# A three-stage attention kernel: new orders for scores, maxima, exponentials, values and the ring of three banks, own PSUM banks for the short rows, and q/k loads a head ahead of v

## What is computed

```python
s = einsum('qd,kd->qk', q, k) * 64 ** -0.5     # forgetting attention: + c[q] - c[k], causal
s = where(mask, s, -inf)                        # sparse: top-256 keys; dilated: three windows
m = max(s, -1); e = exp(s - m); den = sum(e, -1)
o = einsum('qk,kd->qd', e, v) / den
```

## Time and profile before

| what | value |
| --- | --- |
| median of 3 runs | 3623.88 us (3623.08 to 3627.99) |
| the profiled execution | 3628.1 us, its span 3626.3 us |
| mean granted TensorE clock | 0.961 of full |
| TensorE matmul busy | 3270.4 us (90%) |
| TensorE weight load busy | 2684.2 us (74%) |
| VectorE busy | 1818.7 us (50%) |
| ScalarE busy | 1278.6 us (35%) |
| GpSimd busy | 821.7 us (23%) |
| stretch of the FOX stage | about 587 to 765 us |
| stretch of the sparse stage | about 763 to 950 us |
| stretch of the dilated stage | about 2254 to 2596 us |

### The profile page before, as it was taken

The page is one execution under the profiler, slowest core; times in us unless marked ns, Lnnn a source line. Parts: engine busy times, 40 slices in busy tenths (PEclk is TensorE's granted clock), DMA queues, the critical chain, the costliest instruction groups (busy, mean ns, idle before and its releaser), DMA issues. The chain is left out here.

```text
span 3626.3 us, 45156 instructions
## 1 busy us (share of the span) xinstructions
PE 3270.4 (90%) x15622; PEld 2684.2 (74%) x15622; DVE 1818.7 (50%) x3077; ACT 1278.6 (35%) x2732; POOL 821.7 (23%) x509
## 2 busy tenths in 40 slices
PE   8778986969889999999988998799888999999988
PEld 6556875857667888888866886677677888888866
DVE  2398994748424444444442431688524444444342
ACT  3364424747423222222232211677513221222231
POOL 2332264345211000000031441666211000000030
PEclk9899998989989999999999999899998999999999
DMA  4203222212212111111021223222112111111021
GB/s 131 53 16 104 93 90 82 47 41 59 82 47 82 47 35 58 46 35 58 0 76 38 93 98 128 52 49 55 53 42 58 58 46 49 46 44 58 0 76 47
DMA packets 268629, 214.78 MB, mean 59 GB/s; under 512 B 95164, under 2 KB 220908, under 8 KB 268524
## 3 DMA queue, kind: packets, MB, share of 16 engines
q1 hardware_dynamic: 268524, 213.43, 19.9%
HBM read 170.93 MB, written 41.94 MB: 59 GB/s over the span
## 5 line engine op out<-in xcount | busy, mean ns | idle before, releaser
L67 PE MATMUL l0in_acc<-l0in_w_lo,l0h_hi 128*128 128x512 f32 x384 | 151.9, 395 | 25.0 <-POOL l0in_w_lo L1581 25.0
L1655 DVE TENSOR_SCALAR_CACHE_REDUCE k_x<-k_x,l0in_cand 128x384 bf16<-128x384 f32 (+1 forms) x186 | 163.7, 942 | 1.1
L1860 DVE SCALAR_TENSOR_TENSOR l1ff_c<-l1ff_g,l1ff_cw,l1ff_c 128x512 f32<-128x512 f32 x44 | 33.1, 752 | 252.9 <-ACT l1ff_c L1775 252.9
L1860 DVE SCALAR_TENSOR_TENSOR l0ff_c<-l0ff_g,l0ff_cw,l0ff_c 128x512 f32<-128x512 f32 x44 | 33.1, 751 | 251.3 <-ACT l0ff_c L1775 251.3
L131 POOL MEMSET l1pg_mhalf<- 128x8 f32 x1 | 0.1, 105 | 701.1 <-POOLq L106 701.1
L131 POOL MEMSET l0pg_mhalf<- 128x8 f32 x1 | 0.1, 104 | 701.0 <-POOLq L106 701.0
L1881 DVE TENSOR_TENSOR k_x<-l1ff_d,k_x 128x512 f32<-128x512 f32 x176 | 118.0, 689 | 81.0 <-PE l1ff_d L69 81.0
L1881 DVE TENSOR_TENSOR k_x<-l0ff_d,k_x 128x512 f32<-128x512 f32 x176 | 118.0, 689 | 81.0 <-PE l0ff_d L69 81.0
L67 PE MATMUL l1in_acc<-l1in_w_lo,l1h_hi 128*128 128x512 f32 x384 | 150.5, 392 | 5.6 <-POOL l1in_w_lo L467 5.5
L69 PE MATMUL l0in_acc<-l0in_w_hi,l0h_hi 128*128 128x512 f32 x384 | 151.1, 394 | 0.0
L68 PE MATMUL l0in_acc<-l0in_w_hi,l0h_lo 128*128 128x512 f32 x384 | 151.1, 393 | 0.0
(11 more groups left out here) (442 smaller groups left out, 9760.4 us busy)
## 6 DMA issues: line engine op xcount, KB each, us to landing
l0in_raw<-in_w_in_even SPq DMA_DIRECT2D x24, 512.0 KB, 4.0
l1in_raw<-in_w_in_odd SPq DMA_DIRECT2D x24, 512.0 KB, 3.7
l0ff_raw_g<-in_w_gate SPq DMA_DIRECT2D x22, 512.0 KB, 4.1
l0ff_raw_u<-in_w_up SPq DMA_DIRECT2D x22, 512.0 KB, 5.3
l0ff_raw_d<-in_w_down SPq DMA_DIRECT2D x22, 512.0 KB, 4.9
l1ff_raw_g<-in_w_gate SPq DMA_DIRECT2D x22, 512.0 KB, 4.0
l1ff_raw_u<-in_w_up SPq DMA_DIRECT2D x22, 512.0 KB, 5.2
l1ff_raw_d<-in_w_down SPq DMA_DIRECT2D x22, 512.0 KB, 4.8
```

The costliest lines, as they stand in the source:

```text
L67: pe.matmul(out, a_hi, b_lo, start=start, stop=False)
L1655: tick(dve.tensor_scalar(hits[:, cols], score[:, cols], cand[:, i:i + 1].bitcast(F32), 0.0, ALU.is_ge, ALU.add, accum_out=cnt[:, i:i + 1]))
L1860: dve.scalar_tensor_tensor(c[:, half, :], g[:, at - 1:at + 511], cw[:, 1, bass.ds(blk, 1)], c[:, half, :], ALU.mult, ALU.add).then_inc(con ...
```

## The change

The four tables become two named tuples `Order`, one for FOX and one for ROPE, with own tables for scores (`logits`), maxima (`maxima`), exponentials (`exps`), values (`values`) and the copies (`copies`), each of which may name several entries for an item. The row orders become (1, 0, 2, 3), (6, 4, 5, 7) for FOX and (0, 2, 1, 3), (4, 6, 5, 7) for ROPE. A short row gets a bank of its own: the four banks of `ps_s` hold the four short rows of a head, or two long rows. TensorE's wait in front of a row follows from that table of banks (`EXPS_BEFORE`). SyncE loads q and k of head h+3 where it loaded those of h+2; v loads stay a head behind.

```diff
+ROPE_ORDER = Order(
+    rows=((0, 2, 1, 3), (4, 6, 5, 7)),
+    items=[
+        ("q", 0), ("k", 0), ("p", 0, 0), ("p", 0, 1), ("p", 0, 2), ("k", 1), ("f", 1), ("p", 0, 3), ("q", 1), ("p", 1, 0), ("p", 1, 1),
...
+    EXPS_BEFORE = ((-1, -1, 0, 0), (2, 4, 5, 6))
...
-        ps_s = st.ps("s", [P, 2, SEQ])
+        ps_s = st.ps("s", [P, 2 * SEQ])
...
+        def row_at(g, i):
+
+            return i * 512 if g == 0 else i % 2 * SEQ
...
-            with sp.Fori(0, LOOP) as j:
+            sp.wait_ge(raw_free, 1)
+            load(2, 0)
+            with sp.Fori(0, LOOP - 1) as j:
                 for b in range(2):
-                    sp.wait_ge(raw_free, 2 * j + b + 1)
-                    load(2 * j + b + 2, b)
+                    sp.wait_ge(raw_free, 2 * j + (b + 2))
+                    load(2 * j + (b + 3), 1 - b)
                     sp.wait_ge(pv_done, j * 24 + 12 * (b + 1))
-                    load_v(2 * j + b + 2, b)
+                    load_v(2 * j + (b + 2), b)
...
-                    if item in LOGITS_AFTER:
-                        ahead, g, i = LOGITS_AFTER[item]
+                    for ahead, g, i in order.logits.get(item, ()):
                         if not (ahead and last):
-                            if ahead and i == 0:
-                                pe.wait_ge(drained, nth_drained(h, ("k", g)))
-                            pe.wait_ge(exp_done, row_tile(h + ahead, g, i) - 1)
+                            if i == 0 and (ahead or not first):
+                                pe.wait_ge(drained, (h + ahead - 1) * M + (M0 + TURNED_BEFORE[g] + 1))
+                            if ahead or not first or EXPS_BEFORE[g][i] > 0:
+                                pe.wait_ge(exp_done, (h + ahead) * 8 + EXPS_BEFORE[g][i])
```

More of the change, by code:

```diff
@@ L1 @@
+from collections import namedtuple
 from contextlib import ExitStack
@@ L821, in _ @@
                     p_turn(j)
+Order = namedtuple("Order", "rows items logits maxima exps values copies")
+FOX_ORDER = Order(
+    rows=((1, 0, 2, 3), (6, 4, 5, 7)),
+    items=[
+        ("p", 0, 0), ("q", 0), ("p", 0, 1), ("k", 0), ("p", 0, 2), ("k", 1), ("p", 0, 3), ("f", 1), ("c", 0), ("q", 1), ("p", 1, 0),
+        ("p", 1, 1), ("p", 1, 2), ("p", 1, 3), ("p", 1, 4), ("p", 1, 5), ("c", 1), ("p", 1, 6), ("p", 1, 7), ("f", 0)],
+    logits={
+        ("p", 0, 1): ((0, 1, 2),), ("p", 0, 2): ((0, 1, 3),), ("f", 1): ((1, 0, 0),), ("q", 1): ((1, 0, 1),),
+        ("p", 1, 1): ((1, 0, 2), (1, 0, 3)), ("p", 1, 4): ((1, 1, 0),), ("f", 0): ((1, 1, 1),)},
+    maxima={
+        ("q", 0): ((0, 1, 2),), ("p", 0, 2): ((0, 1, 3),), ("c", 0): ((1, 0, 0),), ("p", 1, 1): ((1, 0, 1), (1, 0, 2)),
+        ("p", 1, 4): ((1, 0, 3),), ("c", 1): ((1, 1, 0),), ("f", 0): ((1, 1, 1),)},
+    exps={
+        ("q", 0): ((0, 1, 1),), ("p", 0, 2): ((0, 1, 2),), ("p", 0, 3): ((0, 1, 3),), ("p", 1, 1): ((1, 0, 0),),
+        ("p", 1, 2): ((1, 0, 1),), ("p", 1, 4): ((1, 0, 2),), ("c", 1): ((1, 0, 3),), ("p", 1, 7): ((1, 1, 0),)},
+    values={
+        ("q", 0): ((1, 1, 5),), ("k", 0): ((1, 1, 6), (1, 1, 7)), ("k", 1): ((0, 0, 0), (0, 0, 1)), ("f", 1): ((0, 0, 2),),
+        ("p", 1, 0): ((0, 0, 3),), ("p", 1, 3): ((0, 1, 0), (0, 1, 1)), ("c", 1): ((0, 1, 2), (0, 1, 3)), ("p", 1, 6): ((0, 1, 4),)},
+    copies={
+        ("p", 0, 2): ((1, 1),), ("p", 1, 1): ((0, 0),)})
@@ L827, in attention_stage @@
     FOX = decay is not None
-    ROWS = ((3, 2, 1, 0), (7, 6, 5, 4))
+    order = FOX_ORDER if FOX else ROPE_ORDER
+    ROWS, ITEMS = order.rows, order.items
     KEYS = (4, 8)
     AT = [{t: sum(s + 1 for s in rows[:i]) * P for i, t in enumerate(rows)} for rows in ROWS]
[L831 to L834, removed]
     FIRST = [it for it in ITEMS if it[0] in "qkc"]
@@ L839, in attention_stage @@
     LAST_IN_BANK = [max(n for n in range(N) if n % 3 == b) for b in range(3)]
[L840 to L846, removed]
+    TURNED_BEFORE = [max(DRAINED.index((c, half)) for c in "qk" for half in range(g + 1)) for g in range(2)]
+    EXPS_BEFORE = ((-1, -1, 0, 0), (2, 4, 5, 6))
+    AHEAD = [(g, i) for it in ITEMS for ahead, g, i in order.logits.get(it, ()) if ahead]
+    BACK = [(g, k) for it in ITEMS for back, g, k in order.values.get(it, ()) if back]
     with Stage(nc, name) as st:
@@ L1036, in body @@
                             round_turn(item, 1 - b, n % 3)
-                    if item in EXPS_AFTER:
-                        ahead, g, i = EXPS_AFTER[item]
+                    for back, g in order.copies.get(item, ()):
+                        if not (back and first):
+                            copy_out(h - back, g)
+                    for ahead, g, i in order.exps.get(item, ()):
                         if not (ahead and last):
                             exps(h + ahead, 1 - b if ahead else b, g, i)
[L1041 to L1044, removed]
                 if last:
@@ L1053, in _ @@
                 round_turn(item, 0, n % 3)
-            for i in range(4):
-                exps(0, 0, 0, i)
-            exps(0, 0, 1, 0)
+            for it in ITEMS:
+                for ahead, g, i in order.exps.get(it, ()):
+                    if ahead:
+                        exps(0, 0, g, i)
             heads(act, body)
@@ L1116, in body @@
                             rest_turn(item, 1 - b, n % 3)
-                    if item in LOGITS_AFTER:
-                        ahead, g, i = LOGITS_AFTER[item]
+                    for ahead, g, i in order.maxima.get(item, ()):
                         if not (ahead and last):
-                            if FOX and i == 0:
-                                dve.wait_ge(rounded, nth_rounded(h, turn0[-1] if g == 0 else turn1[-1]))
+                            if FOX and i == 0 and (ahead or not first):
+                                dve.wait_ge(rounded, nth_rounded(h + ahead - 1, ("c", g)))
                             row_max(h + ahead, 1 - b if ahead else b, g, i)
@@ L1132, in _ @@
                 dve.wait_ge(mask_in, 16)
[L1133 to L1136, removed]
+            for it in ITEMS:
+                for ahead, g, i in order.maxima.get(it, ()):
+                    if ahead:
+                        row_max(0, 0, g, i)
             heads(dve, body)
@@ L1170, in logits @@
                     end = min(at + 512, (t + 1) * P)
[L1171 removed]
+                    s = ps_s[:, row_at(g, i) + at:row_at(g, i) + end]
                     q = q2[:, b, t * P:(t + 1) * P]
```

54 lines of the change are left out of this document (34 added, 20 removed), and 3 rows, old and new, of the table values.

## The result

The changed kernel takes 3536.18 us (median of 4 runs, 3531.9 to 3538.31), the kernel before, on the same chip, 3625.93 us (3623.08 to 3632.21). The ratio is 0.9751, with a 95% interval of 0.9739 to 0.9763: faster by 2.5%. I forecast 3560 us with a range down to 3540. The direction held, and so did the main mechanism (the waits for exponentials go), but the gain was larger than my range allowed: on the profiled executions 3628.1 - 3536.72 = 91.4 us instead of 63.9.

A forecast was written before the change was run, and what follows sets the result against it. TensorE was taken to bound the kernel, with waits for exponentials to remove. 22 x 2.46 + 7 x 1.4 = 63.9 us takes the profiled 3628.1 to 3564.2 us, or 3560 us against the median; range 3540 to 3593 us.

The forecast's parts named there:

- What bounds: Whole kernel: TensorE is the busy engine, 90% of the span, losing time mostly to waits for exponentials of short rows.
- ROPE, gain 2.46 us a head: Sparse and dilated stages: waits for exponentials go, so a head falls from 18.96 to 16.5 us, over 22 heads.
- the two engines meeting: ROPE heads: 0.1 us added to the 16.4 us period because TensorE and VectorE are both nearly full.
- fewer changes of kind: TensorE switching between transposes and other matmuls: below 0.1 us left out in ROPE, some 0.2 us saved in FOX.
- the low bound: Whole kernel: no wait left and saved kind changes counted, ROPE heads 16.1 us, FOX heads 17.6 us, giving 3540 us.
- FOX, gain 1.4 us a head: FOX stage: a head falls from 20.17 to 18.8 us, over 7 heads, with two waits left.
- two waits, 0.4 and 0.9 us: FOX heads: 1024-key scores wait 0.4 us for the 640-key row's exponentials; TensorE waits 0.9 us for the outputs' copy.
- First and last body: Ends of each attention stage: preparation bound by GpSimd, less to interleave in the last head; put at 0, within 1 us.
- Loads and GpSimd at nothing: Earlier q/k load lets GpSimd finish `stage` 6 us ahead, costing nothing; beyond that each microsecond late shows in every head.
- VectorE as the bound: Rival: each of 24 rests and maxima a head costs its whole duration, VectorE needs 17.8 us, 3590 us; chance 0.12.
- The waits did not only move: Rival: TensorE's lost time returns at other items, under 7 us gained, 3620 us; chance 0.04.
- the banks did not close up: Rival: score banks must empty and refill once a head, 3.6 us against 2.5 saved, 3658 us; chance 0.05.

The follow-up runs named there:

- The kernel with the order that I had in mind: Changed kernel with FOX's 768-key and 1024-key score rows placed earlier, as the prediction had read the table: 3542.64 us, ratio 0.9770.
- kernel with shared banks: Changed kernel with short rows back in two shared buffers of 1024 columns and four exponentials moved one or two items forward: 3625.19 us, ratio 0.9997.
- the one with only the banks: Old order of everything, with short rows in banks of their own and the earlier q/k loads: 3599.19 us, ratio 0.9920 to the kernel before.
- kernel with fewer groups: Changed kernel with ROPE's values in pairs behind three ring items less: 3537.33 us, ratio 0.9752 to the kernel before.

## Why the prediction failed, point by point

**What bounds.** Right. TensorE was the busy engine with waits for exponentials, and no TensorE wait is left in the steady heads.

**ROPE, gain 2.46 us a head.** The mechanism was right, the size 0.30 us short: 2.76 us, 22 x 0.30 = 6.6 us. I took 16.4 us from the weight loads' waits as TensorE's own time, and added 0.1 us for the two engines meeting. The period is 16.2 us. The waits of PEld in the earlier trace rows still understate the loss by some 0.2 us, and the two engines hardly meet: VectorE is busy for 15.3 us a head and not for the 15.9 us with which I reckoned, and a whole extra rest on it costs 0.2 us. The saving from fewer changes of kind, which I left out here and counted in FOX and in the low bound, is zero.

**FOX, gain 1.4 us a head.** This step failed, by 7 x 0.98 = 6.9 us. I placed the scores of the 768-key row one ring item too early and those of the 1024-key row two when I read the table, and so counted two waits, 0.4 and 0.9 us, that the changed kernel does not have. The kernel with the order that I had in mind has both and runs at 18.9 us. That this is so near my 18.8 us is in part luck: its waits are 1.0 us and not 1.3, the 18.0 us under them should be 17.8, the saving of 0.2 us does not exist, and 18.8 was chosen between two reckonings, 19.1 and 18.5. The changed kernel has three items between these exponentials and scores, and its scores stand in front of the values and hide the copy.

**First and last body, "at 0, within 1 us a stage either way".** This failed too, and is the largest part: 12 us in three stages, 5.1, 3.1 and 3.8. I asked how many heads differ and not what TensorE waits for in the first and the last body. At the start of FOX these are the waits of the earlier trace rows, up to 1.6 us long against 0.8 in a steady head, and more than half of the gain there is busy time at a higher granted clock. In the last heads they are mostly other waits, for `pt_lo` and `o_sb`, which my sum did not have at all. The start of the ROPE stages, where my 0 held, held it by a trade: the shorter waits for exponentials went into 12 more matmuls and a wait for GpSimd.

**Loads and GpSimd at nothing.** Right, and its cover was real. `stage` was done at 2416.02 + 4.59 = 2420.61 and TensorE turned q at 2427.01, 6.4 us later (I had 6). Without the earlier load the time is 141 us more.

**The rivals.** VectorE as the bound did not come: 0.69 us operations start 0.61 us apart, and the heads run at 16.2 us, under the 17.8 us that whole durations would give. The sentence that I drew from the Trainium skill ("VectorE: DVE Perf Modes", section "The DRAIN you can't avoid"), that the next operation does not start until the pipeline is empty, was only half of what the section says: a next operation that is not held, it goes on, starts earlier. The rests and maxima here do. The waits did not only move, and the banks did not close up. The run that did end slower than before did so by the load's place, which I had named under the loads (past its cover each microsecond shows in every head) but not as a rival.

**The range.** 6.6 + 6.9 + 12 + 2 = 27.5 us, the whole miss. My low bound had 80.9 us and 3 for the ends. Steady heads alone, 77.4 us, would have stayed in it; the ends left it.

## What to carry to other kernels

When waits for a buffer are to go, count the distance in items from each release to each use, from the very table that the code runs, and read it twice: scores one and two items too early were 1.1 us a FOX head here. Try more buffers and a new order together: here they gave 27 us and 1 us apart and 90 us as one, and the loads that feed the faster loop had to be moved in the same step. Count the waits of the first and the last copy of a head by themselves; here they were partly other waits than a steady head's, and gave 12 of the 91 us.

## What the runs showed of the hardware that I had not expected

The granted clock at the start of FOX. Before (594 to 603 us), three stretches of 3 us, columns as in the earlier trace rows:

```profile
594.00:597.00 3.00, 1.26 (x7) 0.96 (x7) 1.61 (x5) 2.21 (x5) 2.54 (x3) 0.88 0.01 3
597.00:600.00 3.00, 2.31 (x8) 2.02 (x9) 0.85 (x4) 1.47 (x6) 2.74 (x3) 0.50 0.00 0
600.00:603.00 3.00, 3.00 (x11) 2.52 (x10) 1.29 (x2) 0.07 (x1) 3.00 (x3) 0.50 0.00 0
```

After, the same place:

```profile
595.00:598.00 3.00, 2.60 (x15) 2.22 (x16) 2.11 (x8) 2.81 (x8) 2.54 (x4) 1.00 0.06 11
598.00:601.00 3.00, 2.68 (x21) 2.18 (x19) 2.05 (x4) 1.88 (x5) 2.74 (x2) 1.00 0.00 0
```

Before, TensorE was busy 1.26 of 3 us and then ran at 0.50, the level of 1.2 GHz; a 512-column matmul took 0.42 us to the next start there (600.26 to 600.68) instead of 0.23. After, it was busy 2.60 of 3 us and stayed at 1.00. The kernel with shared banks falls to 0.54 and 0.50 as well, the one with only the banks does not. So at a stage's start the two waits appear to cost more than their own length, through the clock: of the 4.2 us at FOX's start, 2.7 are busy time. No run changes the clock by itself.

The second thing is that a group of transposes of another kind between matmuls is free, by the rows of the kernel with fewer groups: 0.11 us for each transpose, however they are spread.
